# Column sums of five RMSNorms: one fp32 pass of ones, or a split and two fp32r passes inside the second unit

## The reference

```python
def rmsnorm(x, g):
    y = x * rsqrt(mean(x * x, axis=-1) + EPS)
    return y * g

for i in range(2):
    h = h + mixer_i(rmsnorm(h, norm_mix[i]))          # dilated / differential attention
    h = h + squared_relu_mlp(rmsnorm(h, norm_mlp[i]), w_ff1[i], w_ff2[i])
    gate = sigmoid(rmsnorm(h, norm_ple[i]) @ w_ple_gate[i])
    h = h + gate * (p[i] @ w_ple_proj[i])
return rmsnorm(h, final_norm)
```

## Time and profile before

| what | value |
|---|---|
| median of 3 runs | 1620.86 us |
| the profiled execution, its own time | 1621.36 us |
| its span, first to last instruction | 1619.6 us |
| TensorE busy | 1602.7 us (99%) |
| VectorE, ScalarE, GpSimd busy | 911.6, 605.8, 61.0 us |
| mean granted TensorE clock | 0.997 |
| fp32 matmul of ones (L1654) | 10 records, two per norm, 590 to 697 ns each |
| additions on GpSimd (L812) | 41, 1.29 to 1.84 us each |
| table load on ScalarE | 1.28 us |

### The profile page before, as it was taken

How to read it: one execution, slowest core, us unless ns; L and a number is a source line. 1 busy time by engine, 2 the same in 40 slices (tenths; PEclk the granted TensorE clock), 3 DMA queues, 4 the chain that set the end, 5 groups by cost and what they waited for, 6 DMA issues and landing times.

```text
span 1619.6 us, 22080 instructions
## 1 busy us (share of the span) xinstructions
PE 1602.7 (99%) x8243; PEld 1322.0 (82%) x8243; DVE 911.6 (56%) x1597; ACT 605.8 (37%) x1098; POOL 61.0 (4%) x60
## 2 busy tenths in 40 slices
PE   8999999999999999999999999999999999999997
PEld 7888888888888788888888878888878888888886
DVE  5355455455455863635455676777676363535555
ACT  5233334334334431222223445666653131212344
POOL 0000000000000200000001110000020000000111
PEclk9999999999999999999999999999999999999999
DMA  6543443443332333333333333323233333333331
GB/s 160 149 120 92 112 122 90 111 123 83 100 88 69 104 91 100 95 95 95 97 93 101 98 114 89 91 65 100 69 91 94 102 91 104 91 101 93 92 114 69
DMA packets 300572, 160.13 MB, mean 99 GB/s; under 512 B 31545, under 2 KB 295282, under 8 KB 300514
## 3 DMA queue, kind: packets, MB, share of 16 engines
q1 hardware_dynamic: 300112, 158.61, 34.7%
q0 software_dynamic: 144, 0.71, 0.2%
q10 hardware_dynamic: 258, 0.04, 0.0%
HBM read 157.11 MB, written 10.60 MB: 104 GB/s over the span
## 4 chain that ended last, share of the span: by engine, by line
PE 95%; POOL 1%; DVE 1%; ACT 1%; DMA 1%; issue 0%; ACTq 0%; POOLq 0%; SPq 0%
PE unit_out L1583 26%; PE unit_out L1585 26%; PE unit_out L1584 26%; PE turned L1659 2%; PE attn L1725 2%; POOL sumsq L812 1%; PE attn L1964 1%; PE logits L1659 1%; PE unit_out L1744 1%; PE logits L1583 1%; PE unit_out L1745 1%; PE unit_out L1746 1%; PE misc L1659 1%; PE misc L1583 1%; PE misc L1585 1%; PE misc L1584 1%
## 5 line engine op out<-in xcount | busy, mean ns | idle before, releaser
L1583 PE MATMUL unit_out<-act_hi,w_hi 128*128 128x512 f32 x1857 | 730.8, 394 | 1.6 <-DVE act_lo L1147 0.8
L1585 PE MATMUL unit_out<-act_hi,w_lo 128*128 128x512 f32 x1857 | 721.9, 389 | 0.0
L1584 PE MATMUL unit_out<-act_lo,w_hi 128*128 128x512 f32 x1857 | 721.1, 388 | 0.0
L830 ACT ACTIVATE w_hi<-w_raw 128x1024 fp32r<-128x1024 f32 (+3 forms) x257 | 272.0, 1058 | 463.7 <-PE unit_out L1585 348.4
L1583 PEld LDWEIGHTS unit_out<-act_hi,w_hi 128*128 128x128 f32 x1857 | 349.1, 188 | 77.4 <-DVE w_lo L1132 3.9
L1585 PEld LDWEIGHTS unit_out<-act_hi,w_lo 128*128 128x128 f32 x1857 | 348.7, 188 | 72.7
L1584 PEld LDWEIGHTS unit_out<-act_lo,w_hi 128*128 128x128 f32 x1857 | 349.0, 188 | 70.1 <-issue 0.7
L1132 DVE TENSOR_TENSOR w_lo<-w_raw,w_hi 128x1024 fp32r<-128x1024 f32 (+3 forms) x257 | 321.6, 1251 | 119.9 <-ACT w_hi L830 119.8
L989 ACT ACTIVATE act_hi<-hidden 128x512 fp32r<-128x512 f32 x64 | 40.5, 633 | 243.4 <-DVE hidden L1392 243.4
L812 POOL TENSOR_TENSOR sumsq<-sumsq,square 128x512 f32<-128x512 f32 x41 | 57.8, 1410 | 1532.8 <-ACT square L858 1531.1
L1389 DVE TENSOR_TENSOR scaled<-unit_out,rstd 128x512 f32<-128x512 f32 x62 | 42.8, 690 | 67.7 <-PE unit_out L1585 67.7
(11 more groups left out here) (275 smaller groups left out, 1404.7 us busy)
## 6 DMA issues: line engine op xcount, KB each, us to landing
w_raw<-in_w_ff_dram SPq DMA_DIRECT2D x128, 512.0 KB, 4.1
w_raw<-in_a_w_qkv_dram SPq DMA_DIRECT2D x56, 512.0 KB, 3.9
w_raw<-in_b_w_qkv_dram SPq DMA_DIRECT2D x24, 512.0 KB, 5.1
w_raw<-in_a_w_qkv_dram SPq DMA_DIRECT2D x32, 256.0 KB, 3.0
w_raw<-in_w_ple_gate_dram SPq DMA_DIRECT2D x16, 512.0 KB, 4.1
bias_tiles_b<-bias_vectors SPq DMA_DIRECT2D x16, 256.0 KB, 4.4
bias<-bias_tiles_b SPq DMA_DIRECT2D x8, 512.0 KB, 3.8
w_raw<-in_a_w_o_dram SPq DMA_DIRECT2D x8, 448.0 KB, 3.8
```

What stands on the lines that cost most here:

```text
L830: sc.activation(weights_of(u)[0][:, 0:width, :], w_raw[par][:, 0:width, :], ACT.Copy).then_inc(hi_done, 1)
L1583: te.matmul(bank, w_k[0], hi, start=start, stop=False)
L1584: te.matmul(bank, w_k[0], lo, start=False, stop=False)
L1585: return te.matmul(bank, w_k[1], hi, start=False, stop=stop)
```

## The change

`sumsq` is split like every other operand: ScalarE copies it to an fp32r high part (`sumsq_parts[:, 0]`), VectorE subtracts to get the rest (`sumsq_parts[:, 1]`), and TensorE multiplies fp32r ones by both, two passes in place of one fp32 matmul. The sums move on TensorE from behind unit 0 to behind the third slab (9 matmuls) of unit 1. For norms 1, 3 and 4 ScalarE runs a one-element square root ahead of the wait for `sumsq`, which loads the root's table early. `sumsq_parts` lies where `scaled` and `hidden` lie.

```diff
+            def split_sumsq_hi(norm):              # ScalarE
+                if norm % 3 < 2:
+                    sc.activation(spare[:, :], eps_col[:, 0:1], ACT.Sqrt)
+                sc.wait_ge(sumsq_done, norm * KC)
+                sc.activation(sumsq_parts[:, 0, :], sumsq[:, :], ACT.Copy).then_inc(sumsq_hi_ready, 1)
...
+            def split_sumsq_lo(norm):              # VectorE
+                ve.wait_ge(sumsq_hi_ready, norm)
+                ve.tensor_tensor(sumsq_parts[:, 1, :], sumsq[:, :], sumsq_parts[:, 0, :], ALU.subtract
+                                 ).then_inc(sumsq_lo_ready, 1)
...
             def statistics(norm):                  # TensorE
-                te.wait_ge(sumsq_done, norm * KC)
-                te.matmul(attn[:, :], ones[:, :], sumsq[:, :], start=True, stop=True
+                te.wait_ge(ones_ready, 1)
+                te.wait_ge(sumsq_hi_ready, norm)
+                te.matmul(attn[:, :], ones_r[:, :], sumsq_parts[:, 0, :], start=True, stop=False)
+                te.wait_ge(sumsq_lo_ready, norm)
+                te.matmul(attn[:, :], ones_r[:, :], sumsq_parts[:, 1, :], start=False, stop=True
                           ).then_inc(stat_ps, 1)
...
                 def up(u, k, n, is_first):         # TensorE, MLPs
-                    if is_first:
+                    if u.reg is None and n == 1:
+                        unit(u, IN[layer], part=(0, 3))
                         statistics(norm)
-                    else:
+                        unit(u, IN[layer], part=(3, KC)).then_inc(units_done, 1)
+                    elif not is_first:
                         whole(u, IN[layer])
...
                     # TensorE, gates
-                    unit(u, IN[layer], act_ready if n == 0 else None, norm * KC)
+                    if n == 1:
+                        unit(u, IN[layer], part=(0, 3))
+                        statistics(norm)
+                        unit(u, IN[layer], part=(3, KC))
+                    else:
+                        unit(u, IN[layer], act_ready if n == 0 else None, norm * KC)
...
-                    if n == 0:
-                        statistics(norm)
...
                     # TensorE, mixer of layer 1
+                        if first and n == 1 and k == 2:
+                            statistics(3)
                         if k == KC - 1:
                             last.then_inc(units_done, 1)
-                            if first and n == 0:
-                                statistics(3)
```

More of the change, by code:

```diff
@@ L278, in build @@
         square = [sb(f"square{i}", [P, T]) for i in range(2)]
+        with nc.sbuf_tensor("sumsq_parts", [P, 2, T], F32R) as sumsq_parts:
+            pass
         scaled = sb("scaled", [P, T])
@@ L282, in build @@
         ones = sb("ones", [P, P])
+        ones_r = sb("ones_r", [P, P], F32R)
         gains = sb("gains", [P, 64])
@@ L521, in build @@
         act_ready = sem("act_ready")
+        ones_ready = sem("ones_ready")
+        sumsq_hi_ready = sem("sumsq_hi_ready")
+        sumsq_lo_ready = sem("sumsq_lo_ready")
         stat_ps = sem("stat_ps")
@@ L983, in up @@
                         next_hi(u)
+                    if is_first:
+                        split_sumsq_hi(norm)
                     if two_ahead and n < KC - 1:
@@ L1034, in sub_b @@
                     next_hi(u + (0 if i == 0 else 2))
+                    if s.reg is None and s.const == 0 and i == 0:
+                        split_sumsq_hi(3)
                 if not has_proj:
@@ L1174, in split_table @@
                 ve.tensor_copy(table[rows, :], table_rest[rows, :]).then_inc(table_ready, 1)
+            ve.wait_ge(const_ready, 2)
+            ve.tensor_copy(ones_r[:, :], ones[:, :]).then_inc(ones_ready, 1)
             ve.memset(table_in[PIECES:PIECES + 1, :], -MASKED).then_inc(table_ready, 1)
@@ L1383, in up @@
                         next_lo(u)
+                    if is_first:
+                        split_sumsq_lo(norm)
                     if two_ahead and n < KC - 1:
@@ L1476, in sub_b @@
                     next_lo(u + (0 if i == 0 else 2))
+                    if s.reg is None and s.const == 0 and i == 0:
+                        split_sumsq_lo(3)
                 if not has_proj:
```

## The result

The changed kernel takes 1623.79 us, the median of 9 runs (1622.02 to 1626.27); the kernel before took 1620.61 us, the median of 9 (1619.94 to 1622.30). The ratio is 1.0019, with a 95% interval from 1.0011 to 1.0027: 3.2 us longer, just under 0.2%. The median forecast was 1622.7 us, the range 1620.2 to 1624.4. So the median lies in the range, 1.1 us above the forecast; as a difference to the kernel before, 3.2 us were measured where 1.85 were forecast. The profiled execution has 1622.88 us and a span of 1621.1 us, 1.5 us more than before.

What follows compares the result with a forecast made beforehand. TensorE, busy 99% of the span, was taken as the bound. Its shifts at the five norms, +0.455 - 0.41 + 0.8 + 1.0 + 0.0 = +1.85 us, took 1620.86 to 1622.7 us; range 1620.2 to 1624.4.

Steps and rivals of the forecast that it cites:

- The price of the two forms: At norm 2 the fp32 sum costs 0.87 us, two fp32r passes 0.455; straight saving 0.41 a norm.
- Unit 1 starts when `w_lo` is there: Norms 1, 3 and 4: the end of `w_lo`'s subtraction, 2.30 us at 1 and 4, releases unit 1; its start stays.
- Rival A: GpSimd releases unit 1, which starts 1.08 us earlier at norms 1 and 4, 0.23 at 3: 1620.3 us; chance 0.12.
- The root 1.67 us later: Norms 1, 3 and 4: with the passes inside unit 1, the root comes 2.88 us behind its start.
- the three stalls: Behind the late root: 0.4 us at norm 3's scores, 0.45 at norm 4's unit 3, 0.3 at norm 5's unit 2.
- Rival B: What is late behind the root is caught up, only the passes count: +0.5, 1621.4 us; chance 0.15.
- What costs nothing: `sumsq`'s high copy, its rest and the pushed splits stay covered; without that cover, 0.7 to 1.7 us a norm.
- The sum: TensorE's shifts at norms 1 to 5: +0.455, -0.41, +0.8, +1.0, 0.0, together +1.85 us.
- rival D: Clock falls after 1.25 us idle ahead of unit 1 at norms 1 and 4: +5.5, 1626.3 us; chance 0.06.
- the prediction's own sign: The prediction called itself wrong if, among other signs, the granted clock drops at norms 1 and 4.
- Rival C: Every norm gives back the whole sum with its wait: -3.2, 1617.7 us; chance 0.03.

Runs made afterwards that it cites:

- the kernel with fp32 inside: Changed kernel with one fp32 matmul of ones in the new place inside unit 1, splits kept and waited for: 1625.33 us, 4.5 over before.
- the small addition: GpSimd's last addition at norms 1 and 4 over one column: 1619.94 us in the changed kernel, 1619.60 in the kernel before, against 1620.79.
- the kernel that takes them away: Changed kernel with both passes behind the first slab of unit 1 (3 matmuls in place of 9): 1622.20 us, 1.3 over before.
- The filled gap: Changed kernel with ten identity transposes on TensorE ahead of unit 1 at norms 1, 3 and 4: 1622.21 us, 1.3 over before.

## Why the prediction was right, and where it was not

- **The price of the two forms.** 0.455 us for two fp32r passes, 0.87 for the fp32 one: shown, by the cadence around them in three traces and by the kernel with fp32 inside.
- **Unit 1 starts when `w_lo` is there.** Shown. It starts 0.06 us behind it in the changed kernel as well, and earlier only when the addition beside `w_lo` is gone. Rival A, that GpSimd's sum releases it, falls: the wait for GpSimd is gone and unit 1 stands where it stood. The Trainium skill ("SBUF — State Buffer", "Who interferes with whom") has a VectorE instruction with two SBUF inputs contend with a GpSimd instruction that reads SBUF. The trace with the small addition agrees: without GpSimd beside it `w_lo` takes 1.21 us, with it 2.30.
- **The root 1.67 us later, and the three stalls.** Norm 3 moved by 0.97 - 0.21 = 0.76 where 0.8 was forecast, norm 4 by 1.83 - 0.80 = 1.03 where 1.0 was, norm 5 by about 0 as forecast. Rival B, that what is late is caught up, falls by the three waits and by the kernel that takes them away, at norms 4 and 5; at norm 3 the wait goes too, but the wait of the second pass takes its place.
- **What costs nothing.** The copies and the moved splits have no wait in the trace. The early table load gained nothing: the root waits 2.4 us for TensorE at norm 4, with its table long loaded.
- **The sum.** +1.85 was forecast for an execution in which the clock stays; the last instructions of ScalarE are 1.9 us later in the profile, of which 0.16 is there before norm 1, and the span 1.5. Over the stretch from norm 1 on it is +1.75 to +1.91 in the profiles without a fall.
- **Where it was wrong: the step on rival D.** It held one stretch of the kernel before, busy for 0.67, against the fall, and gave it 0.06, as something that happens always or never, at both norms. The runs show it in some executions: behind norm 1 in two of the five profiles of the changed kernel, behind norm 4 in the profile with fp32 inside unit 1. By the prediction's own sign, a drop of the granted clock there, this part of it was wrong. One fall costs 1.6 us. The 1.8 that was priced took the low stretch at the start as 3.6 us long; the granted clocks of its two halves (0.63 from 8 to 10 us, 0.51 from 10 to 12) give 3.4. The fall doesn't begin with the first matmul of unit 1 either, but with the second or third.
- **How much it is.** Two in five of 1.6 us is some 0.6 us, worked out from these profiles; with that as an expected cost the sum would have given some 1623.3. The filled gap gave back 1.3. So this part is shown as to its place and only roughly as to its size. The mean clock of a run doesn't settle it: 8 of the 23 runs of the changed kernel have 0.996 or less, against 3 of the 73 runs of before whose clock was listed, but the profile with fp32 inside unit 1 has a fall and a mean clock of 0.997.
- **What was luck.** The median lies in the range, 0.6 us below its upper bound, but the room above the forecast was kept for longer stalls at norms 3 to 5, and those came as forecast. What filled it, as far as the traces show, are falls of the clock.
- **Rival C** had unit 1's gap vanish; nothing did that but the small addition.

What stays open: how often the clock falls behind the norms, between 52 and 60 us (seen in one profile) and at the last sums, in each kernel; and why single runs of the changed kernel at 0.998 still take 1623.84 and 1624.53 us. The head of the kernel differs between executions by enough to be a part of that, but these runs have no trace.

## What to carry to other kernels

An instruction that stands in a wait is free, and taking it out buys nothing: before costing a removal, find what releases the instruction behind it, and look whether that releaser is itself stretched by a neighbour. Moving work out of a gap and into a dense stretch is paid twice, by its own duration and by whoever waits for its result. And the gap that is left is not neutral: the work that stood in it may have kept TensorE's clock up, as the useless transposes did here.

## What was not expected of the hardware

A gap of 1.25 us, behind a wait of 0.73 and a shorter one at norm 1 and behind two of 0.7 at norm 4, sometimes takes the granted clock to 1.2 GHz and sometimes not, with the same program and the same gaps; a gap of 3.04 us did so at both of its places in the one trace of it. After the 1.25 us gap the fall comes late: in one execution the first two matmuls of unit 1 still ran at full speed and the third was caught in it, and full speed came back some 3.3 us later. Ten useless transposes in each of three gaps, 1.25 us on TensorE each time, made the median 1.3 us shorter. And VectorE's 128x1024 subtraction took 2.30 us beside GpSimd's 128x512 addition and 1.21 without it.
